# Down projection by Strassen's seven products in a convolutional-FFN encoder layer on Trainium2

## The reference

```python
def conv_ffn(x, w_up, conv_w, conv_b, w_down):
    h = x @ w_up                                   # (512, 1024) @ (1024, 5632)
    h = lax.conv_general_dilated(h, conv_w...) + conv_b   # depthwise, width 3, along positions
    a, u = jnp.split(h, 2, axis=-1)                # 2816 features each
    return (jax.nn.gelu(a, approximate=False) * u) @ w_down   # (512, 2816) @ (2816, 1024)
...
x = layer_norm(ALPHA * x + mix, ln1_g, ln1_b)
x = layer_norm(ALPHA * x + conv_ffn(x, w_up, conv_w, conv_b, w_down), ln2_g, ln2_b)
```

## Time and profile before

| what | value |
|---|---|
| time, median of three runs | 1003.73 us (1003.02 to 1004.0) |
| span of the profiled execution, first to last instruction | 1001.4 us |
| median less span | 2.3 us |
| PE busy | 987.4 us, 99% |
| VectorE (DVE) busy | 734.4 us, 73% |
| ScalarE (ACT) busy | 464.8 us, 46% |
| GpSimd (POOL) busy | 220.7 us, 22% |
| chain that ended last | PE 95%, DVE 2%, ACT 2% |

### The profile page before, as it was taken

One profiled execution on the slowest core, in us unless ns is written; L12 is line 12 of the kernel. 1 busy time (PEld: TensorE's weight loads), 2 busy tenths in 40 slices (PEclk: granted clock), 3 DMA queues, 4 the chain that ended last, 5 costly groups with the idle time before them and its releaser, 6 DMA issues.

```text
span 1001.4 us, 12301 instructions
## 1 busy us (share of the span) xinstructions
PE 987.4 (99%) x4614; PEld 824.2 (82%) x4614; DVE 734.4 (73%) x1110; ACT 464.8 (46%) x742; POOL 220.7 (22%) x210
## 2 busy tenths in 40 slices
PE   7999999999999999999999999999999999999997
PEld 6888888998888788888888888888888888888885
DVE  6664567886786898788778778778777394665587
ACT  6574666896313754554554554454457402113000
POOL 2400426774950000000000000000000299500022
PEclk9999999999999999999999999999999999999999
DMA  8334141008240223223222322322339512413022
GB/s 309 95 81 151 43 107 43 1 1 252 85 148 22 84 65 103 82 68 93 76 85 76 92 85 67 103 85 63 105 134 350 209 72 97 169 53 158 1 84 84
DMA packets 91179, 102.11 MB, mean 102 GB/s; under 512 B 20091, under 2 KB 71247, under 8 KB 91120
## 3 DMA queue, kind: packets, MB, share of 16 engines
q1 hardware_dynamic: 89904, 99.15, 30.0%
q10 hardware_dynamic: 1216, 2.17, 0.7%
HBM read 79.29 MB, written 22.02 MB: 101 GB/s over the span
## 4 chain that ended last, share of the span: by engine, by line
PE 95%; DVE 2%; ACT 2%; issue 1%; DMA 0%; POOL 0%; DVEq 0%; SPq 0%; ACTq 0%; POOLq 0%
PE ps L701 31%; PE ps L703 30%; PE ps L702 30%; PE ps L915 1%; PE ps L1044 1%; DVE prob L1377 1%; DVE pTl L1174 1%; ACT prob L1908 1%; PE ps L736 1%; ACT pTh L1731 0%; DMA acc<-in_x_prompt 0%; PE ps L711 0%; PE ps L724 0%; PE ps L884 0%; PE ps L976 0%
## 5 line engine op out<-in xcount | busy, mean ns | idle before, releaser
L701 PE MATMUL ps<-d_hi,g_hi 128*128 128x512 f32 x352 | 137.0, 389 | 0.0
L703 PE MATMUL ps<-d_hi,g_lo 128*128 128x512 f32 x352 | 136.9, 389 | 0.0
L702 PE MATMUL ps<-d_lo,g_hi 128*128 128x512 f32 x352 | 136.9, 389 | 0.0
L668 POOL TENSOR_TENSOR acc<-acc,gain_bc 128x1024 f32<-128x1024 f32 x12 | 32.8, 2732 | 466.2 <-ACT bias_bc L1731 466.2
L702 PEld LDWEIGHTS ps<-d_lo,g_hi 128*128 128x128 f32 x352 | 66.1, 188 | 13.8
L703 PEld LDWEIGHTS ps<-d_hi,g_lo 128*128 128x128 f32 x352 | 66.1, 188 | 13.8
L701 PEld LDWEIGHTS ps<-d_hi,g_hi 128*128 128x128 f32 x352 | 66.1, 188 | 13.7 <-DVE d_lo L1174 0.2
L701 PE MATMUL ps<-x1h,wa_hi 128*128 128x512 f32 x192 | 75.6, 394 | 0.0
L703 PE MATMUL ps<-x1h,w_lo 128*128 128x512 f32 x192 | 74.8, 389 | 0.0
L702 PE MATMUL ps<-x1l,wa_hi 128*128 128x512 f32 x192 | 74.7, 389 | 0.0
L2028 ACT ACTIVATE hc<-U,taps 128x512 f32<-128x512 f32 x60 | 48.7, 813 | 44.7 <-DVE U L1556 41.4
(11 more groups left out here) (298 smaller groups left out, 2740.4 us busy)
## 6 DMA issues: line engine op xcount, KB each, us to landing
w_raw<-in_w_up SPq DMA_DIRECT2D x44, 512.0 KB, 4.7
g_scratch<-gated SPq DMA_DIRECT2D x22, 512.0 KB, 2.6
g_raw<-g_scratch SPq DMA_DIRECT2D x22, 512.0 KB, 6.1
d_raw<-in_w_down SPq DMA_DIRECT2D x22, 512.0 KB, 7.4
acc<-in_x_sample SPq DMA_DIRECT2D x8, 512.0 KB, 12.0
st_raw<-in_w_in SPq DMA_DIRECT2D x16, 256.0 KB
x_scratch<-acc SPq DMA_DIRECT2D x8, 512.0 KB, 3.5
acc<-x_scratch SPq DMA_DIRECT2D x8, 512.0 KB, 7.9
```

The costliest lines, as they stand in the source:

```text
L668: chain.mark(pool.tensor_tensor(dst, dst, gain_bc[:], ALU.mult))
L701: pe.matmul(out, whi, xhi, start=start, stop=False, skip_group_check=onto)
L702: pe.matmul(out, whi, xlo, start=False, stop=False, skip_group_check=onto)
L703: return pe.matmul(out, wlo, xhi, start=False, stop=stop, skip_group_check=onto)
```

## The change

Tokens are the rows of a two by two block matrix (prompt, sample), features a pair of tiles (even, odd), and output columns two halves of 512. For 18 of the 22 tiles (9 pairs, in three groups of 3) the four block products of a pair, eight in number, are replaced by seven of sums, in 21 steps. A step is one of the seven products for three pairs: 4 token tiles by 3 pairs by 3 matmuls. The sums of the gated rows are made by VectorE into `gsum` at the end of each odd tile of the up projection and stored; the sums of the weight blocks are made in DRAM, by copies on SP's queue and accumulating DMAs from GpSimd. Some operands are kept with a negative sign. Four products keep their PSUM banks from the step two before and add to it. The outputs of steps 0, 2, 3 and 6 are copied to `part_sum` by ScalarE, the others added or subtracted by VectorE. Five slots of buffers hold the steps' operands. The last 4 tiles are done as a plain chunk. Several semaphores of the earlier stages are merged, with the same waits.

```diff
+PAIRED = 18
+QUADS = PAIRED // 2
+CHUNK = 3
+STEPS = 7 * (QUADS // CHUNK)
+SLOTS = 5
+LAST = FT - PAIRED
+PRODUCTS = ((X11, B11, True, True), (X12, B21, False, True), (S2, T2, False, False), (S1, T1, False, True),
+            (S3, T3, True, False), (S4, B22, False, False), (X22, T4, True, False))
+TARGETS = ((0, 0, 1), (0, 0, 1), (0, 1, -1), (4, 1, 1), (4, 1, -1), (0, 1, 1), (4, 0, 1))
+def by_act(n):
+    return n in (0, 2, 3, 6)
...
@@ SP @@
             def store_gated(v):
+                g, q = gated[v % 2], v // 2
                 sp.wait_ge(g_ready, 2 * v + 2)
...
+                elif v % 2 == 0:
+                    sp.dma_start(gs_dram[X11, :, q, :], g[:, 0:SEQ]).then_inc(g_out[0], 32)
+                else:
+                    sp.dma_start(gs_dram[X12:X22 + 1, :, q, :].rearrange("i p n -> p i n"), g[:].rearrange("p (i n) -> p i n", i=2)).then_inc(g_out[1], 32)
+                    sp.wait_ge(gs_sum, 4 * (q + 1))
+                    sp.dma_start(gs_dram[S1:S4 + 1, :, q, :].rearrange("i p n -> p i n"), gsum[:]).then_inc(gs_out, 16)
+            def start_weight_sum(j):
+                c, i = divmod(j, 4)
+                src = (quarter[B11], quarter[B22], b12, quarter[B21])[i]
+                sp.dma_start(ts_dram[i, :, quads(c), :], src[:, quads(c), :]).then_inc(ts_copy[c], 16)
+            def load_step(n):
+                c, i = divmod(n, 7)
+                a, w, s = PRODUCTS[i][0], PRODUCTS[i][1], n % SLOTS
+                if i == 0:
+                    for e in range(2):
+                        sp.wait_ge(g_out[e], 32 * CHUNK * (c + 1))
+                    sp.wait_ge(gs_out, 16 * CHUNK * (c + 1))
+                    sp.wait_ge(ts_sum, 64 * (QUADS // CHUNK))
+                if n >= SLOTS:
+                    sp.wait_ge(dn_ps, 4 * (n - SLOTS + 1))
+                sp.dma_start(ga_raw[s][:], gs_dram[a, :, quads(c), :]).then_inc(step_in[s], 16)
+                src = ts_dram[TSUM[w], :, quads(c), :] if w in TSUM else quarter[w][:, quads(c), :]
+                sp.dma_start(db_raw[s][:], src).then_inc(step_in[s], 16)
...
                 elif v + 2 < FT:
                     sp.wait_ge(p_ps[3], v + 1 - PLAIN)
                     load_up(v + 2)
+                    if v - PLAIN < 12:
+                        start_weight_sum(v - PLAIN)
                 elif v + 2 == FT:
                     sp.wait_ge(p_ps[3], v + 1 - PLAIN)
+                    sp.wait_ge(p_ps[1], FT - PLAIN)
+                    load_step(0)
+                    load_step(1)
+                else:
+                    sp.wait_ge(p_ps[4], FT - PLAIN)
+                    load_step(2)
                 store_gated(v)
             sp.wait_ge(p_ps[3], FT - PLAIN)
+            load_step(3)
+            for s in range(2):
+                sp.wait_ge(g_out[s], 16 * FT)
+            load_step(4)
             for t in range(TT):
                 sp.dma_start(acc[:, t, :], x1_dram[t]).then_inc(x_in[t], 16)
...
             sp.dma_start(gain_bc[:], ln1_g.partition_broadcast(P)).then_inc(gb_in, 16)
             sp.dma_start(bias_bc[:], ln1_b.partition_broadcast(P)).then_inc(gb_in, 16)
+            for n in range(SLOTS, STEPS):
+                load_step(n)
...
+            sp.wait_ge(dn_ps, 4 * (STEPS - 4))
+            load_last(0)
+            sp.wait_ge(dn_ps, 4 * (STEPS - 3))
+            load_last(1)
+            sp.wait_ge(dn_ps, 4 * (STEPS - 2))
+            load_last(2)
+            load_last(3)
@@ GpSimd @@
+            def weight_row_sums(c, part):
+                k, w = [ts_dram[i, :, quads(c), :] for i in range(4)], quads(c)
+                if part == 0:
+                    pool.wait_ge(ts_copy[c], 64)
+                    pool.dma_start(k[0], b12[:, w, :], accum_op=ALU.add).then_inc(ts_sum, 16)
+                    pool.dma_start(k[2], quarter[B22][:, w, :], accum_op=ALU.add).then_inc(ts_sum, 16)
+                elif part == 1:
+                    pool.wait_ge(ts_sum, 64 * c + 32)
+                    pool.dma_start(k[1], k[0], accum_op=ALU.add).then_inc(ts_sum, 16)
+                else:
+                    pool.wait_ge(ts_sum, 64 * c + 48)
+                    pool.dma_start(k[3], k[1], accum_op=ALU.add).then_inc(ts_sum, 16)
...
             for t in range(TT):
                 pool.wait_ge(x0_ready, TT + t + 1)
-                pool.wait_ge(dn_free, 16 + 2 * t + 2)
+                if t < TB:
+                    pool.wait_ge(dn_dve, taken(STEPS - 2, t)[1])
+                else:
+                    pool.wait_ge(dn_dve, taken(STEPS - 1, t - TB)[1])
                 pool.tensor_tensor(acc[:, t, :], acc[:, t, :], part_sum[:, t, :], ALU.add).then_inc(x0_ready, 1)
@@ TensorE @@
+            def down_step(n):
+                i, s = n % 7, n % SLOTS
+                fresh = PRODUCTS[i][3]
+                for t in range(TB):
+                    if n >= 2:
+                        act_took, count = taken(n - 2, t)
+                        pe.wait_ge(dn_act if act_took else dn_dve, count)
...
+                    if t == 0:
+                        pe.wait_ge(dn_lo, 2 * n + 2)
+                    tok = slice(t * P, (t + 1) * P)
+                    for q in range(CHUNK):
+                        last = mm3(ps[:, DOWN_BANKS[n % 2][t], :], ga_hi[s][:, q, tok], ga_lo[s][:, q, tok], db_hi[s][:, q, :], db_lo[s][:, q, :],
+                                   fresh and q == 0, q == CHUNK - 1, not fresh)
+                    last.then_inc(dn_ps, 1)
+            def down_last(i):
...
+                for j in range(LAST):
+                    if i == 0:
+                        pe.wait_ge(dn_lo, 2 * STEPS + 2 * j + 2)
+                    last = mm3(ps[:, last_bank(i), :], g_hi[j][:, tok], g_lo[j][:, tok], d_hi[j][:, cols], d_lo[j][:, cols], j == 0, j == LAST - 1)
@@ VectorE @@
+            def row_sums(v):
+                dve.wait_ge(gs_out, 16 * q)
+                dve.wait_ge(g_ready, 2 * v + 2)
+                dve.tensor_tensor(gsum[:, 0], x21, x22, ALU.add).then_inc(gs_sum, 1)
+                dve.tensor_tensor(gsum[:, 2], x11, x21, ALU.add).then_inc(gs_sum, 1)
+                dve.wait_ge(gs_sum, 4 * q + 1)
+                dve.tensor_tensor(gsum[:, 1], x11, gsum[:, 0], ALU.add).then_inc(gs_sum, 1)
+                dve.wait_ge(gs_sum, 4 * q + 3)
+                dve.tensor_tensor(gsum[:, 3], x12, gsum[:, 1], ALU.add).then_inc(gs_sum, 1)
...
+                    if v % 2 and v < PAIRED:
+                        row_sums(v)
...
+            lows = [(0, 0), (0, 1), (1, 0), (1, 1), (2, 0), (2, 1), (3, 0), (3, 1)]
+            for n in range(STEPS):
+                for t in range(TB):
+                    if not by_act(n):
+                        add_step(n, t)
+                    if t % 2 and n + 2 < STEPS:
+                        step_low(n + 2, t // 2)
+                    elif n + 2 == STEPS and t == 3:
+                        last_low(0, 0)
+                        last_low(0, 1)
+                    elif n + 1 == STEPS:
+                        if t == 1:
+                            for j, w in lows[2:5]:
+                                last_low(j, w)
+                        elif t == 3:
+                            for j, w in lows[5:8]:
+                                last_low(j, w)
@@ ScalarE @@
+            for n in range(STEPS):
+                for t in range(TB):
+                    if by_act(n):
+                        take_step(n, t)
+                    if t % 2 and n + 2 < STEPS:
+                        step_high(n + 2, t // 2)
+                if n == 0:
                     act.wait_ge(gb_in, 64)
                     copy(gain_bc[:], gain_bc[:], gb_ready, ALPHA)
                     copy(bias_bc[:], bias_bc[:], gb_ready, ALPHA)
+            for j in range(LAST):
+                for w in range(2):
+                    last_high(j, w)
```

More of the change, by code:

```diff
@@ L106, with taken, x22_negative @@
 PLAIN_BANKS = ((4, 5, 1, 6), (0, 2, 3, 7))
[L108 to L117, removed]
+PAIRED = 18
[4 more added lines that the diff above has]
+LAST = FT - PAIRED
+DOWN_BANKS = ((6, 7, 4, 5), (1, 0, 2, 3))
+X11, X12, X22, S1, S2, S3, S4 = range(7)
+B11, B21, B22, T1, T2, T3, T4 = range(7)
+TSUM = {T1: 0, T2: 1, T3: 2, T4: 3}
+PRODUCTS = ((X11, B11, True, True), (X12, B21, False, True), (S2, T2, False, False), (S1, T1, False, True),
[3 more added lines that the diff above has]
+    return n in (0, 2, 3, 6)
+def taken(n, t):
+    same = sum(1 for k in range(n) if by_act(k) == by_act(n))
+    return by_act(n), 4 * same + t + 1
+def x22_negative(v, b):
+    return v < PAIRED and v % 2 == b
 def slot_count(v, plain, each):
@@ L302, in build @@
[L302 to L312, removed]
+    gsum = at("gsum", [P, 4, 512], F32, 32 * KB)
+    part_sum = at("part_sum", [P, TT, D], F32, R + 98 * KB)
+    SLOT_KB = ((22, 28, 34, 40), (46, 60, 92, 52), (68, 74, 80, 86), (130, 136, 142, 148), (0, 6, 12, 154))
@@ L683, in _ @@
                 ln_rstd(t, TT)
+            def weight_row_sums(c, part):
[10 more added lines that the diff above has]
```

(28 more changed lines are left out.)

310 lines of the change are left out of this document (144 added, 166 removed).

## The result

The changed kernel takes 1024.32 us (median of 4 runs, 1022.70 to 1027.46), the kernel before 1003.71 us (4 runs, 1003.02 to 1004.0): 1.0209 times as long, 95% interval 1.0191 to 1.0227. It is slower, by 20.6 us, clear of no change; whether by more than 2% the interval leaves open. The forecast was slower, 1017 us, range 1000 to 1026. The profiled execution took 1024.54 us, with a span of 1022.7 against 1001.4 before: +21.3 us to explain.

What follows compares the result with a forecast made beforehand. PE's gapless matmuls were taken to bound the kernel; -24.5 + 2 + 17.9 + 15.8 + 2 = +13.2 us on a 1001.4 us span, plus 2.3 us from span to median, gave 1017 us, range 1000 to 1026.

Steps and rivals of the forecast that it cites:

- PE work removed: Down projection: 756 matmuls replace 864, so 108 go, -24.5 us.
- Row sums and copies: Up projection: VectorE's added row sums and the twelve DRAM copies on SP's queue cost nothing.
- Weight sums in DRAM: Up projection: GpSimd's twelve accumulating DMAs may slow w_up loads; taken as +2 us, lower bound 0.
- Rival 4: Accumulates are slow, hit two or more w_up loads a group or hold step 0: 1025 us and up, chance 0.13.
- Hand-over: Up to down projection: loading steps 0 and 1 is hidden; 1.5 us of lateness for step 1 is swallowed.
- The wait that decides: ScalarE, end of step 0: waiting for gain_bc and bias_bc delays step 3 by 17.9 us, bounds 16 to 20.
- GpSimd beside VectorE: Down projection: they take turns, 3.34 us between low parts, yet steps 3 to 10 barely hold PE's pace.
- Rival 1: Broadcast wait bites, tail does not, as VectorE keeps the port: +4.9 for +15.8, 1006 us, chance 0.18.
- The tail: After step 20's end, E: GpSimd's part_sum additions and late low parts delay the last outputs, +15.8 us, upper bound 18.
- Clock: PE idles ahead of step 3, which then starts at half clock: +2 us, bounds 0 and 8.2.
- likeliest case: Whole kernel: the main forecast of 1017 us, own range 1009 to 1024, chance 0.50.
- Rivals 2 and 3: 2: broadcast wait over before step 3, 999 us, chance 0.10; 3: neither broadcast wait nor tail bites, 984 us, 0.09.

Runs made afterwards that it cites:

- e2: The changed kernel with the twelve accumulating DMAs left out, copies, row sums and their stores kept: 1015.47 us, ratio 1.0113 to the kernel before.
- e8: The kernel before with only the twelve weight copies and twelve accumulating DMAs added, their sums unread: 1003.25 us, ratio 1.0002.
- e1: The changed kernel with ScalarE's wait for the two broadcasts moved from behind step 0 to behind step 4: 1005.76 us, ratio 1.0022.
- e6: The changed kernel with SP sending both broadcasts right behind the loads of steps 0 and 1, ScalarE's wait unchanged: 1004.92 us, ratio 1.0017.

## Why the prediction was right

- *PE work removed*, -24.5: 948 matmuls, and steps 4 to 20 without a stall. Right.
- *Row sums and copies*, nothing: right (e2).
- *Weight sums in DRAM*, +2: **the one term that was mis-sized.** It measured +9.4, just over the upper bound for three hits (8.5). That an accumulate can hit a w_up load and that the margin is 1.16 us was in the working; the value was taken near 0 because the engines' mean share was 0.26. But a mean over 355 us says nothing of the 17 us in which two accumulates, a copy, the store of this very change and the load come together. I priced the accumulates against the load alone, and e8 shows that by itself this costs nothing: the store is what I counted as free and did not put into the same stretch. The 2.8 us worked out for one hit was near the 2.34, 2.44 and 2.04 us that TensorE waited; all three groups hit, and half clock behind the first (1.9 us) was in no term. Rival 4 named the mechanism and 1025 us; it had 0.13. It came about through one load a group, and not the two or more that it asked for.
- *Hand-over*, nothing: 9.73 us late at the first down matmul against 9.4 + 0.4 ahead of it. Right.
- *The wait that decides*, +17.9 (16 to 20): measured 17.3; the broadcasts landed 24.2 us after step 3's issue where 24.5 were worked out, ScalarE idled 19.72 us, and e1 and e6 each give it back. As the down projection began 9.73 us later, the times themselves lie some 9 us behind those worked out. The window in which they load ran at 400 GB/s, over the 383 of the calibration and farther still from the 358 of the Trainium skill ("SBUF — State Buffer", Summary), so the measurement decides: the extra 1.5 us by the rule did not come.
- *GpSimd beside VectorE*: the turns hold between adjacent low parts too (3.41, 3.35 and 3.38 us), which no row before had shown. Rival 1 rested on the contrary. The one read port of the Trainium skill ("SBUF — State Buffer", Who interferes with whom) agrees, and so does its rule that whoever issues first has the port: in the rows the one that waits gets it next, each time.
- *The tail*, +15.8: measured 16.6. Output 0's addition started at E + 17.5 (E + 16.1 worked out). The last low part ended at E + 15.7 instead of E + 15.3, and the matmuls behind it ran at half clock (0.63 us each), 1.8 us instead of 0.8; half clock also stretched the next output. VectorE then took 5.60 us a tile, where I had 5.79.
- *Clock*, +2: measured 2.1 behind step 3. What it costs behind the other waits is in their terms; the prediction had nothing for it there.

The mis-sized term moved the time from 1017 to 1024, just outside the likeliest case's own range of 1009 to 1024. The full range held it because its upper end was put there for accumulates that are slow; of the other terms none is off by more than 1 us. Rivals 2 and 3 fell with the gain_bc copy at 796.

## What to carry to other kernels

Before you call a transfer hidden, lay out what moves in the same 20 us, what the change itself adds included, and for how long each lies beside the load that matters; a mean share over the stage hides it (and a share over the 20 us alone does not decide it), and two costs that are each nothing can be 9 us together. Look in each engine's program for a wait that nobody needed early: a change that moves the loads behind it turns it into a stall, and moving the wait or the load by a few lines gives it back. Work removed from the engine that bounds the kernel pays only as far as the others keep its pace: here 24.5 us went, and the same change made it 21 us slower or 15 us faster by where three waits stood.
